# Two halves of a joined block in one order of high and low tiles that alternates from block to block

## What is computed

```python
def swiglu(x, w_gate, w_up, w_down):
    return (jax.nn.silu(x @ w_gate) * (x @ w_up)) @ w_down
...
u = rmsnorm(h, mix_norm[l])
z = u @ w_in[l]
...
ff = jnp.square(jax.nn.relu(x @ w_ff1[l])) @ w_ff2[l]
x = layer_norm(DEEPNORM_ALPHA * x + ff, ln2_g[l], ln2_b[l])
```

## Time and profile before

| | us |
|---|---|
| median of three runs | 2031.81 |
| lowest and highest | 2031.62, 2031.81 |
| span of the profiled execution (first to last instruction) | 2029.4 |
| TensorE busy (matmuls) | 2021.2 |
| TensorE weight loads | 1709.3 |
| VectorE busy | 1384.2 |
| ScalarE busy | 1016.7 |
| GpSimd busy | 93.4 |

### The profile page before, as it was taken

The page is one execution under the profiler, slowest core; times in us unless marked ns, Lnnn a source line. Parts: engine busy times, 40 slices in busy tenths (PEclk is TensorE's granted clock), DMA queues, the critical chain, the costliest instruction groups (busy, mean ns, idle before and its releaser), DMA issues.

```text
span 2029.4 us, 24942 instructions
## 1 busy us (share of the span) xinstructions
PE 2021.2 (100%) x10260; PEld 1709.3 (84%) x10260; DVE 1384.2 (68%) x1618; ACT 1016.7 (50%) x1282; POOL 93.4 (5%) x133
## 2 busy tenths in 40 slices
PE   9999999999999999999999999999999999999998
PEld 7888888888888888888888888888888888888887
DVE  6655686775757676787675667657767577577675
ACT  6444576453445345675453356654534466545331
POOL 1001010000010001100100000000100000000000
PEclk9999999999999999999999999999999999999999
DMA  9655554465556555544566564654755555555552
GB/s 335 212 187 169 176 163 145 163 207 195 192 183 224 190 179 192 166 143 158 194 209 195 167 229 136 206 167 169 243 195 188 188 175 187 167 186 201 193 187 83
DMA packets 225569, 377.73 MB, mean 186 GB/s; under 512 B 6592, under 2 KB 113216, under 8 KB 225456
## 3 DMA queue, kind: packets, MB, share of 16 engines
q1 hardware_dynamic: 221472, 362.64, 54.5%
q0 software_dynamic: 3984, 13.49, 2.2%
HBM read 375.05 MB, written 1.05 MB: 185 GB/s over the span
## 4 chain that ended last, share of the span: by engine, by line
PE 98%; DVE 1%; ACT 0%; issue 0%; DVEq 0%; POOL 0%; ACTq 0%; POOLq 0%
PE pb L1662 64%; PE pb L1673 18%; PE pb L1676 9%; PE pb L1685 2%; PE pb L1731 1%; PE pb L1809 1%; DVE wl L2105 0%; PE pb L1808 0%; PE pb L1796 0%; PE pb L1788 0%; PE pb L1651 0%; DVE lS L2288 0%; PE pb L1655 0%; PE pb L1690 0%; PE pb L1653 0%; PE pb L1833 0%
## 5 line engine op out<-in xcount | busy, mean ns | idle before, releaser
L1886 ACT ACTIVATE wh<-raw 128x2048 fp32r<-128x2048 f32 (+2 forms) x347 | 654.2, 1886 | 623.9 <-PE pb L1662 278.8
L2105 DVE TENSOR_TENSOR wl<-raw,wh 128x2048 fp32r<-128x2048 f32 (+2 forms) x345 | 774.9, 2253 | 150.5 <-ACT wh L1886 149.5
L1662 PE MATMUL pb<-wh,x 128*128 128x512 f32 (+1 forms) x2144 | 651.2, 385 | 0.0
L1662 PEld LDWEIGHTS pb<-wh,x 128*128 128x128 f32 x2144 | 400.7, 188 | 77.8
L1662 PE MATMUL pb<-wl,x 128*128 128x512 f32 (+1 forms) x1072 | 420.9, 393 | 0.1
L1673 PE MATMUL pb<-x,wh 128*128 128x512 f32 x1568 | 397.0, 395 | 0.0
L1673 PEld LDWEIGHTS pb<-x,wh 128*128 128x128 f32 x1568 | 283.3, 189 | 51.9
L1662 PE MATMUL pb<-wl,mh 128*128 128x512 f32 (+1 forms) x740 | 255.7, 391 | 0.0
L1662 PE MATMUL pb<-wh,ml 128*128 128x512 f32 (+1 forms) x740 | 253.6, 388 | 0.0
L1662 PE MATMUL pb<-wh,mh 128*128 128x512 f32 (+1 forms) x740 | 253.5, 388 | 0.0
L1662 PEld LDWEIGHTS pb<-wl,x 128*128 128x128 f32 x1072 | 201.5, 188 | 41.3 <-issue 3.4
(11 more groups left out here) (353 smaller groups left out, 1570.9 us busy)
## 6 DMA issues: line engine op xcount, KB each, us to landing
raw<-in_w_in_dram SPq DMA_DIRECT2D x100, 1024.0 KB, 5.3
raw<-in_w_ff_dram SPq DMA_DIRECT2D x64, 1024.0 KB, 5.3
raw<-in_ffn_w_down_dram SPq DMA_DIRECT2D x44, 1024.0 KB, 5.0
raw<-in_ffn_w_up_dram SPq DMA_DIRECT2D x42, 1024.0 KB, 5.4
raw<-in_ffn_w_gate_dram SPq DMA_DIRECT2D x41, 1024.0 KB, 5.3
raw<-in_w_branch_dram SPq DMA_DIRECT2D x24, 1024.0 KB, 5.0
raw<-in_w_out_dram SPq DMA_DIRECT2D x16, 1024.0 KB, 5.0
raw<-in_w_in_dram SPq DMA_DIRECT2D x4, 832.0 KB, 4.4
```

The lines of the kernel that those rows point to most:

```text
L1662: ins = e.matmul(pb[b][:, 0:c1 - c0], x[:, s, cols], w[:, n, c0:c1], start=(it["first"] and n == 0 and q == 0), stop=(it["stop"] and n == ...
L1886: e.activation(hi, raw, ACT.Copy).then_inc(m.high_done, 1)
L2105: e.tensor_tensor(lo, raw, hi.bitcast(F32), ALU.subtract).then_inc(m.low_done, 1)
```

## The change

The matmuls of a block's two tiles are joined: high tile of both halves, then low tile of both. The next block (`turned`) has the low tiles of both first and then the high tiles of both, and so on in alternation; a token group sets it back. TensorE still has two items per block: i = 0 issues three of the four runs of eight matmuls and i = 1 the last, each with its own signal of completion. Tile 0 is complete after the third run and tile 1 after the fourth. The banks of both tiles are awaited ahead of the first matmul. On main banks the tick between the items stays where it was; for side banks it comes ahead of both.

```diff
+WIDE_ORDER = {False: ((False, 0), (False, 1), (True, 0), (True, 1)),
+              True: ((True, 0), (True, 1), (False, 0), (False, 1))}
...
+        self.turned = False
...
     def group(self, jobs, start=False, end=False):
 
+        self.turned = False
         idx = [self.take(j["key"]) for j in jobs]
...
         need = self.need("X", range(8), [0, 1])
+        if banks[0] >= 4:
+            self.tick()
+        uses = [self.use(b) for b in banks]
         for i in range(2):
-            if i:
+            if i and banks[0] < 4:
                 self.tick()
-            use = self.use(banks[i])
-            v = self.pe("wide", j=j, i=i, use=use, need=need)
-            epi(i, v["p"], use)
+            v = self.pe("wide", j=j, i=i, uses=uses, need=need, turned=self.turned)
+            epi(i, v["p"], uses[i])
+        self.turned = not self.turned
         self.freed[j] = self.x_free = v["p"]
         self.tick()
...
         elif k == "wide":
             hi, lo = m.weights(it["j"])
-            bank, c = pb[use[0]], slice(i * P, i * P + P)
             pe.wait_ge(m.low_done, it["j"] + 1)
             pe.all_ready(it["need"])
-            pe.wait_ge(m.evac[use[0]], use[1])
-            for s in range(8):
-                e.matmul(bank[:, :], hi[:, s, c], m.x2[:, s, :, :].rearrange("p a s -> p (a s)"), start=(s == 0),
-                         stop=False, skip_group_check=True)
-            for s in range(8):
-                ins = e.matmul(bank[:, 0:S], lo[:, s, c], m.xh[:, s, :], start=False, stop=(s == 7),
-                               skip_group_check=True)
+            if i == 0:
+                for b, g in it["uses"]:
+                    pe.wait_ge(m.evac[b], g)
+            steps = WIDE_ORDER[it["turned"]]
+            for low, q in steps[0:3] if i == 0 else steps[3:4]:
+                b, c = pb[it["uses"][q][0]], slice(q * P, q * P + P)
+                first = low == it["turned"]
+                for s in range(8):
+                    if low:
+                        ins = e.matmul(b[:, 0:S], lo[:, s, c], m.xh[:, s, :], start=(first and s == 0),
+                                       stop=(not first and s == 7), skip_group_check=True)
+                    else:
+                        ins = e.matmul(b[:, :], hi[:, s, c], m.x2[:, s, :, :].rearrange("p a s -> p (a s)"),
+                                       start=(first and s == 0), stop=(not first and s == 7), skip_group_check=True)
             ins.then_inc(m.pe_done, 1)
```

## The result

The changed kernel takes 2035.39 us (median of 14 runs, 2035.1 to 2035.93), the kernel before 2031.38 (14 runs, 2031.13 to 2031.88): 4.0 us more. The ratio is 1.002, with a 95% interval of 1.0013 to 1.0027. The forecast was 2033.7 with a range of 2030 to 2038. It had added +1.9 us to the 2031.81 of three runs; so the difference came out 2.1 us above the forecast, and the time 1.7 us above.

A forecast was written before the change was run, and what follows sets the result against it. TensorE was taken to bound the kernel, through the distance between matmul starts and its waits. Terms of -2.5, +3.4 and +1.0 sum to +1.9 us on 2031.81, so 2033.7 us, range 2030.0 to 2038.0.

The forecast's parts named there:

- Term 1: Joined blocks on TensorE: fewer high runs behind low matmuls, each such run costing about 0.028 us; -2.5 us.
- the 14 others: Low runs in the kernel before that are followed by 512-wide work of other lines, counted as 14.
- Rival A: Matmul order in joined blocks gains nothing while the bank waits stay: +4.4, 2036.2 us; chance 0.12.
- Term 2: Early wait for tile 1's bank: +3.4 us at w_ff1_2's second part, +1.0 us behind the second mixer's gelu group.
- The 0.4 us in hand: FFN's first side block: its bank, used by the first up block's middle transposes, is still emptied 0.4 us early.
- Term 3: Tile 0 ends later in its block, so VectorE's reduce can be up to 1.8 us later; covered by slack, nil.
- Term 4: Side work in the middle of main-bank blocks comes three quarters in; scores still fit: 0, bounds 0 and 1 us each.
- rival B: Second mixer's scores wait for ScalarE's copy, up to 1 us at each of four: 2037.7 us; chance 0.12.
- Term 5: Side-bank blocks tick before, not between, their tiles; only ScalarE and VectorE queue entries come earlier: nil.
- within 0.2%: Whole kernel within 4.06 us of before, about what a measurement can tell from no change; chance 0.70.
- one of my own signs of being wrong: The prediction would be wrong if TensorE waited at places other than the four expected blocks.
- the four: Blocks expected to wait: w_ff1_2's second part (1.7 us) and the second mixer's first joined block behind gelu, twice each.

The follow-up runs named there:

- experiment 3: Changed kernel with each bank awaited where it is first written and zmix moved ahead of the second mixer's last joined block: 2028.58 us, ratio 0.9986.
- experiment 9: Kernel before with only zmix's middle tick moved ahead of the second mixer's last joined block: 2031.25 us, ratio 0.9998.
- experiment 5: Kernel of experiment 3 without alternation, every block with its high tiles first (joined, never turned): 2030.17 us, ratio 0.9993.
- experiment 6: Kernel before with each high matmul followed by the low one of the same rows inside a tile: 2036.49 us, ratio 1.0024.
- experiment 1: Changed kernel with each bank awaited ahead of the first run that writes it, not both ahead of the block: 2031.0 us, ratio 0.9998.
- experiment 4: Kernel before, matmul order kept, with both banks awaited at the block's start and the tick ahead for side banks: 2036.15 us, ratio 1.0022.
- experiment 2: Changed kernel with only zmix's middle tick moved ahead of the second mixer's last joined block: 2033.25 us, ratio 1.0008.
- experiment 8: Kernel of experiment 1 with the middle after two runs instead of three and both reduces waiting for the block's end: 2034.54 us, ratio 1.0015.

## Why the prediction was right, and where it was short

- *Term 1, order, -2.5.* Right: 2.5 us in the trace of the changed kernel, 2.4 to 2.5 by experiments 3 and 9, nearly all of it from joining and little from turning (experiment 5). The counts under it hold too: in the trace of the changed kernel 49 runs of highs stand right behind lows where it was 145, none of the 14 others is left, and 18 runs of lows stand behind side work, where I took 16. (There are 16 runs of blocks, not 12; 12 of them start right behind a token group. All are even, so the 49 stands.) The price is one for a run of highs that stands behind lows; experiment 6 shows that it is no fee of each switch, and it held here since every run is at least eight long. Rival A (nil) is out. By the formula of the Trainium skill (TensorE: Matmul & The Clock Gate, Back-to-back issue gap), a high would follow after an estimated 216 ns and a low after 109; experiment 6 has 236 and 117 between neighbours of the other kind, the runs 227 and 120. The formula has no term for the neighbour, and the trace disagrees with it in size and in that the neighbour counts. I read it too broadly, though: that section gives it for the gap of a matmul in isolation and says that in a stream of weight loads and matmuls both set the distance.
- *Term 2, early bank waits, +3.4 and +1.0.* Right: 1.71, 1.72, 0.47 and 0.50 us in the trace, 4.4 to 4.6 together by experiments 1 and 4. The small parts held as well: from the end of the releasing instruction to the block's first matmul it is 0.145 us at all four, where I had 0.05 + 0.1. The 0.4 us in hand that I gave the side bank of the earlier trace rows is 0.3 in experiment 3, and experiment 5 shows a wait there. The rows to read were the end of VectorE's add and ScalarE's gelu against the block's start, not the wait list, which had nothing.
- *Term 3, tile 0 later, nil.* Right in the changed kernel: with the edits of experiments 1 and 2 only the order's gain is left. Experiments 5 and 8 show that the cover is thinner than I said at a few places.
- *Term 4, side work in the middle, 0.* Here the sum fell short, by 2.0 us. I followed the side work that has less room behind it until the next side work (the scores), and found rightly that it fits. I didn't follow zmix, whose successor on TensorE isn't the next piece of side work but the decay matmuls 8.4 us on, at the end of a VectorE chain without slack. The row that said so was in my own list: the earlier trace rows, which I used only for the 0.05 us of a handover, shows TensorE waiting for lrR. The price of rival B, up to 1 us at four places, was of the right kind, but at the wrong place and with a chance of 0.12.
- *Term 5, ticks ahead for side banks, nil.* No sign of it in the units' steps.

With term 4 at +2.0 the sum is 3.9 us, and 4.0 was measured. The sign and the size of the two terms priced were right, the centre was 2 us low. That the range held the result was luck in part: it reached that high for the sake of A and B, and neither happened. 4.0 us is at the edge of what I called within 0.2% (4.06 us). And one of my own signs of being wrong came true: TensorE waited at places other than the four, behind the last joined block of the second mixer in each layer.

## What to carry to other kernels

When work is moved on the engine that sets the time, list every place where that engine already waits in the kernel before, however short the wait: behind it is a chain with no slack, and each microsecond that the chain's start is moved later comes out whole. When two units of work are joined, keep each one's waits at its own first write; here that alone was worth 4.4 us, more than the better order brought. A change whose gain and new waits cancel to "no difference" can hold a faster kernel (2028.58 us) once they are pulled apart.

## What the runs showed of the hardware that was not expected

The long wait of experiment 8 cost more than its length. Windows around it, with the busy times of the engines and then the granted clock, DMA share and GB/s:

```profile
1456.00:1459.00 3.00, 0.95 (x7) 0.58 (x5) 2.96 (x4) 2.22 (x3) 0.00 (x0) 1.00 0.41 102
1459.60:1462.40 2.80, 2.74 (x7) 2.19 (x8) 2.80 (x5) 0.73 (x2) 0.00 (x0) 0.50 0.44 178
1462.40:1466.00 3.60, 3.60 (x17) 3.02 (x16) 2.35 (x2) 0.00 (x0) 0.00 (x0) 0.97 0.02 5
```

After a wait of 2.7 us (1456.35, four transposes, nothing until 1459.66) the clock was 0.50 for 2.8 us, which is 1.2 GHz, and matmuls started 0.43 to 0.56 us apart instead of 0.23: 1.4 us lost on top of the 2.9 us step. The waits of 1.6 us in the changed kernel left it at 1.00:

```profile
1491.60:1495.00 3.40, 3.33 (x15) 2.76 (x16) 0.52 (x1) 0.53 (x1) 0.00 (x0) 1.00 0.74 299
```

A matmul's distance to the next depends on its neighbour: 236 ns for 512 columns behind 256, 227 behind its like, 117 for 256 columns behind 512, 120 behind its like. I don't know why; that weight loads run at their own pace in the low runs (0.12 us apart) is a guess that experiment 6 did not bear out in size, and no run here tells more.
